# Query and key columns of two attentions: three 256-column products per weight tile in place of one of 512 and one of 256

## What is computed

```python
z = rms_norm(x, mix_norm[l]) @ w_in[l]                # zq: the first 512 columns, self-attention's queries
s = jnp.einsum("bqhcd,bkhcd->bhcqk", qb, k).astype(jnp.float32) * scale
hq = (rms_norm(x, xa_norm[l]) @ xa_wq[l])             # cross queries, 1024 columns
kv = rms_norm(mem, mem_norm[l]) @ xa_wkv[l]           # the first 1024 columns are memory's keys
s = jnp.einsum("bqhd,bmhd->bhqm", hq, mk).astype(jnp.float32) * (XA_HD ** -0.5)
```

## Time and profile before

| what | value |
|---|---|
| timed runs, median (lowest to highest) | 1126.62 us (1126.31 to 1126.67) |
| profiled execution, span | 1124.5 us |
| TensorE, granted clock | 0.999 of full speed |
| TensorE busy | 1117.8 us, 99% of the span, 8266 matmuls |
| VectorE busy | 829.3 us, 74% |
| ScalarE busy | 625.5 us, 56% |
| chain that ended last | TensorE 99% of it |

### The profile page before, as it was taken

One profiled execution on the slowest core, in us unless ns is written; L12 is line 12 of the kernel. 1 busy time (PEld: TensorE's weight loads), 2 busy tenths in 40 slices (PEclk: granted clock), 3 DMA queues, 4 the chain that ended last, 5 costly groups with the idle time before them and its releaser, 6 DMA issues.

```text
span 1124.5 us, 19625 instructions
## 1 busy us (share of the span) xinstructions
PE 1117.8 (99%) x8266; PEld 1051.6 (94%) x8266; DVE 829.3 (74%) x1116; ACT 625.5 (56%) x859; POOL 27.5 (2%) x50
## 2 busy tenths in 40 slices
PE   9999999999999999999999999999999999999998
PEld 9999999888899999999999999988889999888886
DVE  7766667899977785655686675579998778866764
ACT  6554555547756654444574554465577656645454
POOL 1000000100000000000000000010010100000000
PEclk9999999999999999999999999999999999999999
DMA  8965654644544366555547655554546444556561
GB/s 271 325 209 190 221 174 166 217 155 155 186 164 173 113 234 223 173 198 192 205 158 246 217 185 191 188 176 165 185 150 212 163 151 148 194 196 212 183 194 54
DMA packets 66280, 211.16 MB, mean 188 GB/s; under 512 B 5009, under 2 KB 24081, under 8 KB 61073
## 3 DMA queue, kind: packets, MB, share of 16 engines
q1 hardware_dynamic: 65216, 209.19, 54.7%
q10 hardware_dynamic: 976, 0.73, 0.2%
HBM read 208.85 MB, written 1.05 MB: 187 GB/s over the span
## 4 chain that ended last, share of the span: by engine, by line
PE 99%; DVE 0%; ACT 0%; issue 0%; ACTq 0%; DVEq 0%
PE G L1905 10%; PE G L1906 10%; PE G L1907 10%; PE G L1931 8%; PE D L1737 8%; PE D L1736 8%; PE D L1744 8%; PE G L1939 4%; PE G L1841 4%; PE G L1704 4%; PE G L1708 4%; PE G L1707 4%; PE D L1841 3%; PE G L1850 2%; PE D L1782 2%; PE D L1781 2%
## 5 line engine op out<-in xcount | busy, mean ns | idle before, releaser
L1116 DVE TENSOR_TENSOR w_lo<-w_raw,w_hi 128x2048 fp32r<-128x2048 f32 (+3 forms) x260 | 452.6, 1747 | 108.8 <-ACT w_hi L680 107.6
L680 ACT ACTIVATE w_hi<-w_raw 128x2048 fp32r<-128x2048 f32 (+3 forms) x260 | 383.2, 1481 | 168.8 <-PE G L1907 112.1
L1905 PE MATMUL G<-a,w_hi 128*128 128x256 f32 x990 | 273.8, 277 | 0.3 <-DVE w_lo L1116 0.3
L1907 PE MATMUL G<-a,w_lo 128*128 128x256 f32 x990 | 273.3, 276 | 0.0
L1906 PE MATMUL G<-a,w_hi 128*128 128x256 f32 x990 | 273.3, 276 | 0.0
L1905 PEld LDWEIGHTS G<-a,w_hi 128*128 128x128 f32 x990 | 185.8, 188 | 0.7 <-DVE w_lo L1116 0.5
L1906 PEld LDWEIGHTS G<-a,w_hi 128*128 128x128 f32 x990 | 185.8, 188 | 0.0
L1907 PEld LDWEIGHTS G<-a,w_lo 128*128 128x128 f32 x990 | 185.8, 188 | 0.0
L1744 PE MATMUL D<-hT_hi,w_lo 128*128 128x256 f32 x528 | 145.7, 276 | 0.0
L1736 PE MATMUL D<-hT_hi,w_hi 128*128 128x256 f32 x528 | 145.7, 276 | 0.0
L1737 PE MATMUL D<-hT_lo,w_hi 128*128 128x256 f32 x528 | 145.7, 276 | 0.0
(11 more groups left out here) (297 smaller groups left out, 1776.6 us busy)
## 6 DMA issues: line engine op xcount, KB each, us to landing
w_raw<-w_dram SPq DMA_DIRECT2D x120, 1024.0 KB, 5.0
w_raw<-w_dram SPq DMA_DIRECT2D x143, 512.0 KB, 5.2
m_raw<-memT_dram SPq DMA_DIRECT2D x2, 1024.0 KB, 9.2
w_raw<-w_dram SPq DMA_DIRECT2D x6, 256.0 KB, 6.1
w_raw<-w_dram SPq DMA_DIRECT2D x8, 128.0 KB, 4.4
vx<-mem_dram SPq DMA_DIRECT2D x1, 1024.0 KB, 11.9
out_dram<-vx SPq DMA_DIRECT2D x3, 256.0 KB, 2.1
m_raw<-x_dram SPq DMA_DIRECT2D x2, 256.0 KB, 4.6
```

Of the source, the lines that this page charges most:

```text
L680: A(w_hi[:, part_hi(i)], w_raw[:, part(i)], ACT.Copy).then_inc(s_hi, 1)
L1116: V.tensor_tensor(w_lo[:, part_lo(i)], w_raw[:, part(i)], w_hi[:, part_hi(i)].bitcast(F32), ALU.subtract).then_inc(s_lo, 1)
L1905: M(out, whi[:, w], a_hi[:, k, :], start=(k, u) == (0, 0), stop=False, skip_group_check=True)
L1907: last = M(out, wlo[:, w], a_hi[:, k, :], start=False, stop=k == KD - 1, skip_group_check=True)
```

## The change

Weight tiles of these blocks are multiplied as in `gate_up`: high by high, high by low and low by high, 256 columns each, one after the other into one half of a bank. A block of two tiles then fills one bank where it filled two, and ScalarE's copy and VectorE's subtraction read the whole bank; VectorE's drain and addition go. The banks are named anew; key blocks get four banks, so blocks 2 and 3 no longer wait for `kvlo0` and `kvlo1`. Key block 2 (`head_columns_high_first`) still starts on the high weights while the low ones are not yet written. `between` is called after five of the eight slices (30 matmuls). The high weights of these blocks are now moved by 16 elements, as the low ones were.

```diff
-    return stage in ("out", "o")
+    return stage in ("out", "o", "q") or (stage == "kv" and piece < 4) or (stage == "in" and piece in (7, 8))
...
-        K_BANKS = (DD[:, 2:4, :], GG[:, 0:2, :])
+        K_BANKS = (DB[2], G[0], DB[3], G[1])
...
-        HQ = (GG[:, 0:2, :], GG[:, 2:4, :], DD[:, 0:2, :], DD[:, 2:4, :])
+        HQ = (G[0], G[1], DB[0], DB[2])
...
-        Q_BANKS = (GG[:, 2:4, :], GG[:, 0:2, :])
+        Q_BANKS = (G[2], G[0])
...
-                    A(kx_hi[:, 2 * i:2 * i + 2, :], K_BANKS[i % 2][:, :, 0:T], ACT.Copy
+                    A(kx_hi[:, 2 * i:2 * i + 2, :], pair(K_BANKS[i]), ACT.Copy
...
-                    V.tensor_tensor(kx_lo[:, k, :], K_BANKS[i % 2][:, :, 0:T], kx_hi[:, k, :].bitcast(F32), ALU.subtract)
-                    dve.drain()
-                    V.tensor_tensor(kx_lo[:, k, :], K_BANKS[i % 2][:, :, T:], kx_lo[:, k, :].bitcast(F32), ALU.add
+                    V.tensor_tensor(kx_lo[:, k, :], pair(K_BANKS[i]), kx_hi[:, k, :].bitcast(F32), ALU.subtract
                                     ).then_inc(att_dve.sem, att_dve.one(f"kvlo{i}"))
...
+            def head_columns(hi, lo, whi, wlo, bank, ks, width, at=0, ready=None, between=None):
+
+                for k in ks:
+                    if k == KD // 2 + 1 and between is not None:
                         between()
+                    if ready is not None:
+                        pe.wait_ge(s_alo, ready + k + 1)
+                    for d in range(2):
+                        out = bank[:, d * T:(d + 1) * T]
+                        w = slice((k - ks[0]) * width + at + d * P, (k - ks[0]) * width + at + (d + 1) * P)
+                        M(out, whi[:, w], hi[:, k, :], start=(k, d) == (0, 0), stop=False, skip_group_check=True)
+                        M(out, whi[:, w], lo[:, k, :], start=False, stop=False, skip_group_check=True)
+                        last = M(out, wlo[:, w], hi[:, k, :], start=False, stop=k == KD - 1, skip_group_check=True)
+                return last
+
+            def head_columns_high_first(hi, lo, i, bank):
+
+                whi = high_weights_of(i)
+                for k in range(KD):
+                    for d in range(2):
+                        ...
+                        M(out, whi[:, w], hi[:, k, :], start=(k, d) == (0, 0), stop=False, skip_group_check=True)
+                        M(out, whi[:, w], lo[:, k, :], start=False, stop=False, skip_group_check=True)
+                whi, wlo = weights(i)
+                for k in range(KD):
+                    for d in range(2):
+                        ...
+                        last = M(bank[:, d * T:(d + 1) * T], wlo[:, w], hi[:, k, :], start=False, stop=k == KD - 1,
...
-                    if i in (2, 3, 4, 6):
-                        pe.wait_ge(att_dve.sem, att_dve.at(l, f"kvlo{(0, 0, 0, 1, 2, 0, 3)[i]}"))
+                    if i in (4, 6):
+                        pe.wait_ge(att_dve.sem, att_dve.at(l, f"kvlo{i // 2}"))
```

More of the change, by code:

```diff
@@ L133, in lo_is_shifted @@
         return True
-    return hi_is_shifted(name) or stage == "q" or (stage == "kv" and piece < 4) or (stage == "in" and piece in (7, 8))
+    return hi_is_shifted(name)
 def movement(name, shifted):
@@ L851, in q_hi @@
                     act.wait_ge(s_blk, INDEX[l, "in", 0] + 8 + ch)
-                    A(qk_hi[:, 2 * ch:2 * ch + 2, :], Q_BANKS[ch][:, :, 0:T], ACT.Copy
+                    A(qk_hi[:, 2 * ch:2 * ch + 2, :], pair(Q_BANKS[ch]), ACT.Copy
                       ).then_inc(att_act.sem, att_act.one(f"q{ch}"))
@@ L1026, in hq_hi_part @@
                         act.wait_ge(s_blk, INDEX[l, "q", 0] + 3 + h)
-                    A(hq_hi[:, 2 * h:2 * h + 2, :], HQ[h][:, :, 0:T], ACT.Copy).then_inc(xa_act.sem, xa_act.one(f"hq{h}"))
+                    A(hq_hi[:, 2 * h:2 * h + 2, :], pair(HQ[h]), ACT.Copy).then_inc(xa_act.sem, xa_act.one(f"hq{h}"))
                 def exp(h):
@@ L1385, in q_lo @@
                     h = slice(2 * ch, 2 * ch + 2)
-                    V.tensor_tensor(qk_lo[:, h, :], Q_BANKS[ch][:, :, 0:T], qk_hi[:, h, :].bitcast(F32), ALU.subtract)
-                    dve.drain()
-                    V.tensor_tensor(qk_lo[:, h, :], Q_BANKS[ch][:, :, T:], qk_lo[:, h, :].bitcast(F32), ALU.add
+                    V.tensor_tensor(qk_lo[:, h, :], pair(Q_BANKS[ch]), qk_hi[:, h, :].bitcast(F32), ALU.subtract
                                     ).then_inc(att_dve.sem, att_dve.one(f"qlo{ch}"))
@@ L1567, in hq_lo_part @@
                     k = slice(2 * h, 2 * h + 2)
-                    V.tensor_tensor(hq_lo[:, k, :], HQ[h][:, :, 0:T], hq_hi[:, k, :].bitcast(F32), ALU.subtract)
-                    dve.drain()
-                    V.tensor_tensor(hq_lo[:, k, :], HQ[h][:, :, T:], hq_lo[:, k, :].bitcast(F32), ALU.add
+                    V.tensor_tensor(hq_lo[:, k, :], pair(HQ[h]), hq_hi[:, k, :].bitcast(F32), ALU.subtract
                                     ).then_inc(xa_dve.sem, xa_dve.one(f"hq{h}"))
@@ L1829, in first_blocks @@
                     wide(l, "in", i, a_hi, a_lo, G[0:2], range(2 * i, 2 * i + 2), ready=8 * q)
[L1831 to L1859, removed]
-                        between()
[L1861 to L1867, removed]
@@ L1875, in first_queries @@
                     for h in range(2):
-                        last = head_columns(a, whi, wlo, (2 * h, 2 * h + 1), G, range(2 * i, 2 * i + 2), N, ready=8 * q,
-                                            low_first=h == 1)
+                        last = head_columns(a_hi, a_lo, whi, wlo, HQ[h], range(2 * i, 2 * i + 2), N, at=h * T,
+                                            ready=8 * q if h == 0 else None)
                         if (i, h) == (3, 0):
@@ L1884, in queries @@
                 whi, wlo = weights(INDEX[l, "q", 2 + h])
-                head_columns(a, whi, wlo, (0, 1), (DB[0:2], DB[2:4])[h - 2], range(KD), T, between=between).then_inc(s_blk, 1)
+                head_columns(a_hi, a_lo, whi, wlo, HQ[h], range(KD), T, between=between).then_inc(s_blk, 1)
             def gate_up_blocks(l, f, c):
@@ L2118, in self_queries @@
                     whi, wlo = weights(INDEX[l, "in", 7 + ch])
-                    head_columns(a, whi, wlo, (0, 1), (G[2:4], G[0:2])[ch], range(KD), T).then_inc(s_blk, 1)
+                    head_columns(a_hi, a_lo, whi, wlo, Q_BANKS[ch], range(KD), T).then_inc(s_blk, 1)
                 self_queries(0)
@@ L2194, in kv @@
                     if i == 2:
-                        at = INDEX[l, "kv", i]
-                        head_columns(m, high_weights_of(at), w_lo[:, part_lo(at)], (0, 1), DB[2:4], range(KD), T, low=at
-                                     ).then_inc(s_blk, 1)
+                        head_columns_high_first(m_hi, m_lo, INDEX[l, "kv", i], K_BANKS[i]).then_inc(s_blk, 1)
                         return
@@ L2200, in kv @@
                         whi, wlo = weights(INDEX[l, "kv", i])
-                        head_columns(m, whi, wlo, (0, 1), (DB[2:4], G[0:2])[i % 2], range(KD), T, low_first=i == 1
-                                     ).then_inc(s_blk, 1)
+                        head_columns(m_hi, m_lo, whi, wlo, K_BANKS[i], range(KD), T).then_inc(s_blk, 1)
                         return
```

6 lines of the change are left out of this document (5 added, 1 removed).

## The result

The changed kernel takes 1128.77 us (median of 10 executions, 1128.24 to 1129.66), the kernel before 1126.29 beside it (10 executions, 1125.65 to 1126.67): 1.0023 times as long, interval 1.0015 to 1.0031. It is 2.5 us slower where 1.3 us faster had been forecast, and it lies 1.1 us above the end of the range.

The account below looks back on a forecast made before the run. TensorE, with almost no waits, was taken as the bound, so matmul-to-matmul steps set the time. Each layer gains 1.24 - 0.60 = 0.64 us, two layers 1.28: 1126.62 - 1.28 = 1125.3 us, range 1124.7 to 1127.7.

Parts of the forecast that it names:

- the cost of the form: Edited blocks, each layer: 1.24 us of excess over 340.0 ns a tile goes, 0.60 us of entries stays, 0.64 us gained.
- The entries behind scores, transposes, products of probabilities and mean squares: Six starts of narrow streams a layer, each with a first step 0.10 us longer: 0.60 us a layer.
- VectorE, waits, banks: Each edited block loses a VectorE drain and addition, 15.2 us in the launch; costed at nothing; no wait added.
- Moving `between`: `between` comes at 3.40 us into its block instead of 3.17; costed at nothing, at most 0.2 us a layer.
- The rival of the freed VectorE: VectorE's lost work shortens the launch by more, at most 2.5 us faster, 1124.1 us; gain beyond 2 us, chance 0.05.
- The rival of the load side: 320 more weight loads on TensorE, loads already 94% busy, become the bound; priced as the slow step, no chance of its own.
- The first rival: Narrow streams settle at a slower step, 4.4 ns more a matmul: chance 0.24 in some streams, 0.06 in nearly all.
- fast streams: The forecast itself: edited narrow streams run at 113 ns a matmul, 1.28 us faster, 1125.3 us; chance 0.62.
- the partial rival: Slower step only in edited streams entered from other than transposes: 2.2 us, 1127.5 us; chance 0.24 for some streams.
- the 290 from which the rival decides the sign: Number of slow matmuls, of 960 edited, from which the slower step cancels the gain: 1.28 us / 4.4 ns.
- the gain of 1.28: Edited blocks of both layers: 0.64 us a layer from excess that goes, less entries that stay, 1.28 us faster.
- The fixed cost per matmul: Rival: each matmul has a fixed cost hidden by width switches; 1.4 us over 320 tiles, 1126.7 us; chance 0.03.

Follow-up runs that it names:

- e9: Changed kernel with four added matmuls a layer, two of 256 and two of 512 columns, ahead of `pv(2)`: 1128.4 us, ratio 1.0019.
- e1: The changed kernel run again, nothing edited, against the kernel before: 1129.08 us, ratio 1.0026.
- e4: Changed kernel with high and low weights of the edited blocks moved by 48 elements instead of 16: 1129.99 us, ratio 1.0033.

## Why the prediction was wrong

**Right: the cost of the form.** Where a stream is fast, the blocks cost nearly what the sum says. The second layer's keys are 0.17 us shorter (0.21 predicted: 0.51 of excess less three entries of 0.10), the cross queries up to the mean squares 0.19, and the keys alone leave the time at 0.9999. The entries behind scores, transposes, products of probabilities and mean squares, bounded from 0.0 to 0.2 and taken at 0.10, are 0.09 to 0.12: the first step is 0.20 to 0.23 where 0.113 follows.

**Right: VectorE, waits, banks.** VectorE fell by 13.1 us (14 named), TensorE's list of waits is the same, and giving the work back changed nothing. Moving `between` cost nothing that shows. The rival of the freed VectorE is out. The rival of the load side was said to show as the slow step. The number of loads alone does not make that step: key blocks 0 and 1, with the same loads, took 11.42 us in one execution and 11.01 in another.

**Right about the step, wrong about its chance and its streams: the slow step.** The first rival described what happened, with its step of 117.7 ns from the earlier trace rows and its price of 4.4 ns a matmul. The forecast gave it 0.30 against 0.62 for fast streams. The step that failed is the choice between the earlier trace rows for the entries of which the trace had no row: I took the fast entry "since the nearest rows are of the new form". But the earlier trace rows are of that form too, and the trace of before had more on entries of another kind: the cross scores shown under e9, slow behind wide matmuls. Nor did carry over to its own kind of entry: in the changed kernel the first layer's key block 2 and the stream from `pv(2)` start behind four transposes, with the same first step of 0.20 us, and ran at 117.8 ns, while key block 3, behind products of probabilities, where the rival looked for the slow step, was fast. Self block 7, which was on nobody's list as it has no interruption ahead, was slow too. So the kind of interruption does not tell the step, as the forecast and the partial rival both took it to do. And "in the same placement that the change gives these blocks" was taken as a reason against the slow step; the runs show that the placement of 16 allows the fast step and does not give it. In the changed kernel's profile 342 of 480 edited narrow matmuls are slow in the first layer (48 + 48 + 96 + 48 + 102) and 198 in the second, 540 of 960, beyond the 290 from which the rival decides the sign: 540 x 4.5 ns = 2.4 us against the gain of 1.28, about 1.1 us slower. With the first layer's keys fast, as in e1, it is 396 of them and 0.5 us.

**Wrong: where it ends.** The rival was priced on the edited matmuls alone, up to 4.2 us; that is the second step that failed. I had the earlier trace rows before me, "the stream doesn't recover until the next transposes", and did not ask what a changed stream does to those behind it. The slow step was there in blocks that no line of the diff names, 242 and 144 matmuls of cross output and FFN, 1.67 us, and that carried the time out of the range. With it the sum is 0.5 + 1.7 = 2.2 us slower with the first layer's keys fast and 1.1 + 1.7 = 2.8 with them slow; the medians differ by 2.5.

**The fixed cost per matmul** fell: where a stream is fast, a tile of three costs 340.0 ns after as before, and the loss comes and goes in streams whose number of matmuls is the same. The rule that the prediction cited (the Trainium skill, "TensorE: Matmul & The Clock Gate", "Back-to-back issue gap", where it stands for the gap of an isolated matmul) gives 256 / 2.4 + 2.5 = 109.2 ns, neither of the two steps.

**Open.** Why one interruption leads to the one step and another to the other is not settled. The first steps of the two entries shown, 366.28 and 367.63, are alike to 0.01 us, and self block 7 turns slow at its first matmul, out of a fast stream and with nothing between (217.01). So a mere change of blocks can be such an entry. In e4 the step changed in the same way in the other direction, from slow to fast at the scores `S(1)`. Why the place of the weights matters no run measured, and the new PSUM banks were never tried without the new form, though they can't be the whole of it, since one program showed both steps on the same banks. The traffic beside the stream does not tell the steps apart: from `pv(2)` on the DMA moved 116 GB/s before and 115 after, and VectorE was busy for 74% of the stretch in both. And since the added four did not bring block 8 of the second layer to the fast step, there is a part of the state that I did not find. None of the kernels beats the one before: the keys alone come closest, and their 0.3 us is not measurable.

## What to carry to other kernels

Where TensorE is full and every matmul brings its own weights, read the step from start to start in each stream, and not only in the one whose form you copy: if the trace shows two steps for one form, price the edit at both, and count the streams behind it too, edited or not. A change of form can move unedited work; compare stage by stage over the whole launch. Matmuls between streams are not only overhead: here two narrow and two wide ones ahead of a stream brought it to the fast step in 13 of 14 cases where the weights' place allowed it.

## What was not expected of the hardware

A stream of 256-column matmuls with a load each holds 113.3 or 117.8 ns a step at a granted clock of 0.999, for hundreds of matmuls (242 from `pv(2)` on: 27.53 and 28.58 us), and the step can differ between two layers of one execution and between two executions of one program (key blocks 0 and 1: 11.42 and 11.01 us).

A move of the high weights by 16 elements is worth 0.20 us in 48 matmuls behind the same four (5.66 us unmoved against 5.46). The Trainium skill, "TensorE: Matmul & The Clock Gate", "Step-by-step: what each phase is for", says that loading the next weights takes no read bandwidth from the running matmul, since each has a port of its own. The pair of traces does not show what was read when, but it does show that where the loaded operand lies in SBUF bears on the step, by 4%.

Behind the added two narrow and two wide matmuls a stream was fast in 13 of 14 cases in the two kernels whose weights lie as in the changed one, and in none of 12 with them unmoved.
